# Order of the attention units in a fused encoder-layer kernel: by sequence first, or by head pair first

## The reference

```
MLA : 8 heads, query/key width 96, value width 64
      o = softmax(q k^T * 96^-0.5) v
diff: 4 heads, two maps of width 64 each, value width 128
      a = softmax(q1 k1^T / 8) - lam * softmax(q2 k2^T / 8)
      o = rmsnorm(a v) * subln * (1 - lambda_init)
```

## Time and profile before

| | |
|---|---|
| runs | 790.09, 791.55, 792.91 us; median 791.55 |
| profiled execution | 792.64 us, its span 790.9 us |
| busy over the span | PE 734.5 us (93%), DVE 296.9 (38%), ACT 220.0 (28%), POOL 202.2 (26%) |
| mean granted PE clock | 0.976 of full speed |
| attention stage | from 211.9 us (first score) to about 369 us of the span |

### The profile page before, as it was taken

One profiled execution on the slowest core, in us unless ns is written; L12 is line 12 of the kernel. 1 busy time (PEld: TensorE's weight loads), 2 busy tenths in 40 slices (PEclk: granted clock), 3 DMA queues, 4 the chain that ended last, 5 costly groups with the idle time before them and its releaser, 6 DMA issues. The chain is left out here.

```text
span 790.9 us, 12092 instructions
## 1 busy us (share of the span) xinstructions
PE 734.5 (93%) x3874; PEld 407.8 (52%) x3875; DVE 296.9 (38%) x812; ACT 220.0 (28%) x595; POOL 202.2 (26%) x479
## 2 busy tenths in 40 slices
PE   8999999999888999998999983999997999999995
PEld 4555554444465666665455552545543554545532
DVE  2442211010278888881544562212211111211136
ACT  3543220110267766672211110111111111111123
POOL 1232422210024230232101134442332434342110
PEclk9999999999989999999999985999999999999999
DMA  9703002000230000000693148999999689999548
GB/s 339 273 0 107 0 1 106 1 0 1 94 125 1 2 1 1 2 2 0 285 425 142 54 165 317 400 414 418 414 416 413 246 293 413 419 414 402 223 177 316
DMA packets 36888, 154.64 MB, mean 196 GB/s; under 512 B 9653, under 2 KB 10805, under 8 KB 23905
## 3 DMA queue, kind: packets, MB, share of 16 engines
q1 hardware_dynamic: 28112, 136.50, 43.5%
q0 software_dynamic: 7648, 15.76, 5.3%
q10 hardware_dynamic: 1072, 1.70, 0.6%
HBM read 142.29 MB, written 20.03 MB: 205 GB/s over the span
## 5 line engine op out<-in xcount | busy, mean ns | idle before, releaser
L1497 PE MATMUL banks<-arena 128*128 128x512 f32 (+1 forms) x384 | 161.7, 573 | 3.2 <-issue 1.9
L1760 PE MATMUL banks<-arena 128*64 128x256 f32 x1280 | 149.5, 387 | 7.1 <-issue 4.4
L1760 PEld LDWEIGHTS banks<-arena 128*64 128x64 f32 x1280 | 94.2, 139 | 55.6 <-issue 12.3
L1497 PEld LDWEIGHTS banks<-arena 128*128 128x128 f32 x384 | 71.0, 190 | 79.6 <-issue 79.6
L1653 PE MATMUL banks<-arena 128*128 128x512 f32 x192 | 86.4, 598 | 1.1 <-DVE arena L1240 1.1
L1769 PE MATMUL banks<-arena 128*64 128x512 f32 x320 | 79.9, 610 | 1.2 <-ACT arena L1032 0.9
L1196 DVE TENSOR_REDUCE arena<-banks 128x1 f32<-128x512 f32 (+1 forms) x96 | 55.2, 599 | 50.6 <-PE banks L1569 43.2
L1399 DVE TENSOR_TENSOR arena<-arena,banks 128x128 f32<-128x128 f32 x40 | 11.6, 290 | 159.4 <-ACT arena L1024 150.5
L955 ACT ACTIVATE arena<-banks,arena 128x512 f32<-128x512 f32 (+1 forms) x96 | 58.3, 613 | 44.5 <-DVE arena L1199 21.9
L1653 PEld LDWEIGHTS banks<-arena 128*128 128x128 f32 x192 | 35.1, 190 | 38.8 <-issue 37.5
L1024 ACT ACTIVATE arena<-banks 128x128 f32<-128x128 f32 x40 | 11.1, 279 | 156.3 <-PE banks L1760 144.2
(11 more groups left out here) (202 smaller groups left out, 876.8 us busy)
## 6 DMA issues: line engine op xcount, KB each, us to landing
arena<-w_gate SPq DMA_DIRECT2D x32, 1024.0 KB
arena<-w_up SPq DMA_DIRECT2D x32, 1024.0 KB
arena<-w_down SPq DMA_DIRECT2D x32, 1024.0 KB
arena<-w_in SPq DMA_DIRECT2D x3, 2048.0 KB, 8.3
arena<-pair_rows SPq DMA_DIRECT2D x5, 1024.0 KB, 12.3
arena<-w_out SPq DMA_DIRECT2D x1, 4096.0 KB, 12.9
arena<-x SPq DMA_DIRECT2D x6, 512.0 KB, 11.0
h_rows<-arena POOLq DMA_DIRECT2D x6, 512.0 KB, 8.0
```

What stands on the lines that cost most here:

```text
L1497: last = nc.tensor.matmul(bank(mm % 2)[:, 0:GROUP_COLS[g]], xgT[:, t, c, :], w[:, c, :], start=(c == 0), stop=(c == DC - 1))
L1760: last = nc.tensor.matmul(bank(b)[h * SLOTS:(h + 1) * SLOTS, 0:2 * P].rearrange("p (g n) -> p g n", g=2), x_eT[i][:, 2 * (c % 4) + c // 4, ...
```

## The change

The list of units runs by head pair first: for each `j` the prompt's four units, then the sample's eight, four times over. The number of units, their instructions and all shapes stay. The batch numbers, the count of scaled tiles that `transpose_o` waits for, and the waits ahead of the output projection follow the new order; `batch` still counts in the order in which batches run, and prompt and sample batches alternate.

```diff
@@ units()
     out = []
-    for seq0, nt in ((0, 2), (2, 4)):
-        for j in range(4):
+    for j in range(4):
+        for seq0, nt in ((0, 2), (2, 4)):
             for qt in range(nt):
                 out += [(seq0, nt, "mla", j, qt), (seq0, nt, "diff", j, qt)]
     return out
@@ batch(u)
-    return j + (4 if seq0 else 0)
+    return 2 * j + (1 if seq0 else 0)
@@ transpose_o(u)
-                pe.wait_ge(od_scaled, 2 * (b + 1) if b < 4 else 8 + 4 * (b - 3))
+                pe.wait_ge(od_scaled, 6 * (b // 2) + (6 if b % 2 else 2))
@@ out_part(t, part)
                         pe.wait_ge(wout_in, 16)
-                        pe.wait_ge(odT_ready, 4)
-                        pe.wait_ge(o_mla, len([u for u in range(N_UNITS) if is_mla(u) and UNITS[u][0] == 0]))
+                        pe.wait_ge(odT_ready, 7)
+                        pe.wait_ge(o_mla, max(BEFORE[u] for u in range(N_UNITS) if is_mla(u) and UNITS[u][0] == 0) + 1)
```

## The result

The changed kernel took a median of 799.11 us in 9 runs (794.25 to 802.17), the kernel before 792.76 us in the 9 runs beside it (788.39 to 793.61). The ratio is 1.0086, with a 95% interval of 1.0059 to 1.0113: the change is **slower by about 6.5 us**. In the experiments, one of the 12 executions of a_spare256 took 960.15 us at a mean granted clock of 0.743; its ratio leaves it out, and the median of the other eleven is 794.28.

A forecast was written before the change was run, and what follows sets the result against it. Waits decide in the prompt's part; a PE, DVE and ACT loop holds sample rounds at 6.79 us. Rounds from unit 3 to 47 sum to 141.0 us against 136.5, +4.5 on 791.55: about 796.0 us, range 792.8 to 800.5.

The forecast's parts named there:

- The main term: At sample batches' output transposes followed by prompt units, PE waits about 1.75 us for POOL; net +1.4 us, three times.
- the slack: At the transposes behind the delayed MLA score, 0.37 us of PE earliness and 0.17 us between matmuls absorb part of the wait.
- the present crossing: The old order's single passage from prompt to sample units (unit 15 to 17), a round of 5.03 us.
- P2 to S1: Round from a block's second prompt round to its first sample round, between diff scores; taken as 4.7 us.
- The prompt rounds: Rounds from a block's first to second prompt unit, and from there to its first sample unit, taken as 4.7 us each.
- the start: Unit 3 to 5 in the slow clock, with a sample's score as score 4: 7.8 us for 6.65, +1.1 us.
- Rival (a): The new waits at sample batches' transposes bring down the clock: +1.2 to 1.7 us per fall, 797.5 to 801.1; chance 0.25.
- Rival (b): POOL's lateness at the sample batches is absorbed, waits under 0.5 us cost nothing net: +0.3 us, 791.9; chance 0.13.
- Rival (c): Faster: prompt batches' POOL waits vanish, none replace them, and prompt rounds take 4.32 us: -3.1 us, 788.5; chance 0.05.
- Rival (d): POOL waits are longer as PE arrives earlier after a crossing of 4.3 us; gain and wait cancel, inside the forecast.

The follow-up runs named there:

- a_spare256: Changed kernel with three spare 128x256 matmuls on PE ahead of its wait at the output transposes of the first three sample batches; median 794.37 us, ratio 1.0028.
- a_newton1: Changed kernel with one Newton step in place of three in POOL's reciprocal root, so a shorter POOL chain; median 802.11 us, ratio 1.0115 to the kernel before.
- a_lag8: Changed kernel with output transposes eight iterations behind the batch's last unit in place of six; median 791.57 us, ratio 1.0012 to the kernel before.
- a_lag8_fill: Changed kernel with a lag of eight in place of six and two spare matmuls at the stage's end; median 791.99 us, ratio 1.0011 to the kernel before.
- b_lag8_fill2: Kernel before with a lag of eight in place of six and two spare matmuls at the stage's end, repeat run; median 788.88 us, ratio 0.9983.
- a_pool_long: Changed kernel with POOL's chain longer by four repeated instructions per batch; median 810.60 us, ratio 1.0264 to the kernel before.

## Why the prediction was right

**What failed first in the program was named rightly.** The main term was a wait of 1.75 us for POOL, three times, at the transposes of sample batches followed by prompt units, none at prompt batches. It was 1.48, three times, and none. Its net cost over a crossing without the wait was put at 1.4 us, in the round of the wait alone. Against a_newton1, which has the transposes in the same place and no wait, a_spare256 with no fall has 132.7 - 128.7 = 4.0 us more, 1.3 each: 1.09 in the round with the wait (7.74 for 6.65), and 0.25 in the next (7.04 for 6.79). (Against a_lag8, which has the transposes elsewhere too, it is 4.3 us.)

**The step that failed** is the slack, and the round behind. The prediction let 0.37 + 0.17 us of the wait be absorbed and took the next round at 6.79, at no cost. In the round of the wait PE does catch up 0.4 us of the 1.48, but the next round takes 0.25 of that back, so only some 0.15 are absorbed. The timeline of DVE in the changed kernel shows how, beside PE's row at 311.80 above:

```profile
307.21 0.75 DVE L1232 TENSOR_SCALAR arena<-banks,arena 128x512 f32<-128x512 f32 x1 [0.89 <-PE banks L1636]
...
308.93 0.69 DVE L1196 TENSOR_REDUCE arena<-banks 128x1 f32<-128x512 f32 x1 [0.17 <-PE banks L1569]
...
310.96 0.69 DVE L1224 COPY arena<-banks 128x512 f32<-128x512 f32 x1
311.57 1.28 DVE L1196 TENSOR_REDUCE arena<-banks 128x1 f32<-128x512 f32 x2
```

The output copy itself has time, as the prediction said: behind it DVE still waits 0.17 us for the late MLA score's second map. But the mixing and the copy at 310.96 hang on that map, and the next diff score, which PE issued at 310.14, finds DVE busy with them. Its maxima start 1.43 us behind it, where the earlier trace rows have 306.99 - 305.83 = 1.16, and the loop that sets a round is longer by the difference. That 1.4 was forecast and 1.3 measured is in part luck: wait and slack were both taken too large. The two rounds together were forecast at 14.73 us and took 14.78. The prediction's own bounds for the term, 0.7 and 1.8, come out of its figures as 0.9 and 1.9; nothing hangs on it.

**The wait was 0.27 us shorter** than forecast because the chain took 7.2 us for 7.46 (one scaling group of 2.63 for 2.84), and it started 1.3 us behind P2's diff score (260.02 - 258.70) where the present crossing gave 1.87; P2 to S1, shorter than I took, ate most of that.

**The prompt rounds and the start** were forecast at 4.7, 4.7 and 7.8 and came at 4.74, 4.49 and 7.63. The sum of the rounds without the fall, 142.0 - 1.6 = 140.4 us, stands against 141.0 forecast. The +1.1 us at the start holds only where the clock is slow there; in the two profiles that kept it (a_lag8_fill, b_lag8_fill2) it is 5.03 for 4.57, 0.46 us.

**Rival (a) came on top.** It had a chance of 0.25, and it happened: one fall at a wait in both profiles, worth 1.6 us, inside the 1.2 to 1.7 I gave one. The step of the prediction that fell short is the claim that a wait "must be met by little other work" and so would seldom bring one. So the total was near for reasons that partly cancel. Without falls the change is worth less than the forecast of +4.5: the rounds of a_spare256 come to +2.8 from unit 5 to 47, with 1.0 at the start +3.8, and its median to +2.7. The falls then put more on top than the one at a wait that a profile shows, and the measured +0.86% is 6.8 us. Of the 3.1 us between the forecast of 796.0 and the 799.11, 1.2 are the level: the nine runs of the kernel before have a median of 792.76, where the three that I started from had 791.55. The range, 792.8 to 800.5, held the 799.11.

The rule of the Trainium skill that I had set beside this rival (TensorE: Matmul & The Clock Gate, "Why this matters for your kernels") ties the loss of the clock to one long unbroken gap. By that rule the waits never cost the clock. The runs disagree: it fell at waits of 1.48 and 2.61 us, and behind two of 0.72 and 1.10 us with matmuls between.

**Rival (b)**, lateness absorbed, fell: of the 1.48 us some 0.15 were absorbed. **Rival (c)** would have needed the distance that only the longer lag gives; with it (a_lag8) the rounds do come out 1.5 us under the kernel before, and the time still doesn't (ratio 1.0012): the start costs about 1 us where the clock is slow, and its executions spend 39 us at half clock for 37 in the kernel before. Its other price, prompt rounds of 4.32, was wrong: they stayed at 4.74 and 4.49 without any wait. **Rival (d)** was right in kind: P2 to S1 ran at 4.49.

What stays open: why of three waits alike only the first met a fall in both profiles (with the longer waits of a_pool_long the first two did), and where in a typical execution the falls lie. By the mean clocks the changed kernel has about 3.5 to 6 us more at half clock than the kernel before (40 and 43 for 37), one to two falls of 3.4 us.

## What to carry to other kernels

When work is reordered under a fixed lag, ask of every producer that runs beside it how long its chain is in us, and how long the lag is in the *new* neighbours: a lag counted in iterations shrinks when the iterations behind it get smaller. Price a wait on TensorE twice, once for itself and once for the clock that may fall behind it; if the wait can't be removed, a few spare matmuls that end before it does can be worth more than they look. And before moving an instruction by one iteration, look which loop and which PSUM bank it lands in: the lag of 7 removed the wait and was the slower.

## What the hardware showed that wasn't expected

Short waits bring down the clock. It fell to half at a single wait of 1.48 us, and behind 0.72 and 1.10 us of waiting at the stage's end, but not in every execution: the kernel before has the same two waits and kept it, and an idle time of 2.15 us in the drain brought a fall in both profiles of the changed kernel and none in those of a_spare256 and a_newton1. A fall of 3.4 us in a sample round cost 1.6 us, one of 6.8 us about 2.5.

A changed number of small POOL instructions, fewer or more, went with 8 to 10 more packets on an instruction queue (ten for one in the expert stage), far behind the place of the edit, and with about 10 us more (447.8 and 448.3 us behind the last diff score, for 436.5 to 439.3 in all other kernels). An edit of the program's length can so hide what it does in its own stage; the rounds told what the total did not.

A float32 matmul of 128x512 with an identity as weights took 0.89 us between starts (two matmul instructions; 2.68 us for three), twice what I had assumed from the rows; one of 128x256 took 0.52 us (1.56 for three).
